# A decoder step's attention with its fills ordered by first use, and its softmax sums inverted inside it and loaded broadcast by the last projection

## What is computed

```
def one_block(args):
    q_i, cq_i, blk = args
    s = jnp.einsum('bqhd,bkhd->bhqk', q_i, k).astype(jnp.float32) * ATTN_SCALE
    s = s + cq_i[..., :, None] - ck[:, :, None, :]
    q_pos = blk * Q_BLOCK + jnp.arange(Q_BLOCK)
    mask = key_pos[None, :] <= q_pos[:, None]
    p = jax.nn.softmax(jnp.where(mask, s, -jnp.inf), axis=-1)
    return jnp.einsum('bhqk,bkhd->bqhd', p.astype(v.dtype), v)
...
yp = yp + (att * jax.nn.silu(g)) @ w_out1
```

## Time and profile before

| | us |
|---|---|
| median of 3 runs | 3041.19 (3039.72 to 3047.91) |
| profiled execution | 3042.56 |
| its span | 3040.8 |
| granted TensorE clock, mean | 0.967 of full |

### The profile page before, as it was taken

One profiled execution on the slowest core, in us unless ns is written; L12 is line 12 of the kernel. 1 busy time (PEld: TensorE's weight loads), 2 busy tenths in 40 slices (PEclk: granted clock), 3 DMA queues, 4 the chain that ended last, 5 costly groups with the idle time before them and its releaser, 6 DMA issues. The chain is left out here.

```text
span 3040.8 us, 46331 instructions
## 1 busy us (share of the span) xinstructions
PE 2789.8 (92%) x17133; PEld 2224.5 (73%) x17133; DVE 1592.0 (52%) x2154; ACT 1026.1 (34%) x1725; POOL 1377.5 (45%) x986
## 2 busy tenths in 40 slices
PE   3899999869989999999999739999999999998999
PEld 3899999757749989999899725555555555554887
DVE  4244333343545789865555465555645555453432
ACT  4333325312452222221122104454444455444100
POOL 0000000010003885469999836777776777776000
PEclk9999999979999999999999959999999999999999
DMA  4101111055635888788888767787897877874531
GB/s 122 44 28 47 46 35 37 14 182 173 183 119 170 293 288 276 252 276 272 268 261 275 220 152 221 207 242 217 218 252 205 240 211 221 238 212 140 168 119 63
DMA packets 327914, 547.68 MB, mean 180 GB/s; under 512 B 76093, under 2 KB 220129, under 8 KB 319212
## 3 DMA queue, kind: packets, MB, share of 16 engines
q1 hardware_dynamic: 246604, 454.31, 50.7%
q10 hardware_dynamic: 78080, 75.65, 7.6%
q0 software_dynamic: 3008, 14.81, 1.3%
HBM read 449.58 MB, written 95.12 MB: 179 GB/s over the span
## 5 line engine op out<-in xcount | busy, mean ns | idle before, releaser
L1174 POOL TENSOR_TENSOR p_kq<-p_kq 128x1024 f32<-128x1024 f32 x256 | 624.4, 2465 | 373.9 <-DMA p_kq<-in_cache_k_dram 373.5
L2037 POOL TENSOR_TENSOR at_acc<-at_acc,at_w 128x512 f32<-128x512 f32 (+3 forms) x576 | 645.2, 1120 | 229.5 <-ACT at_w L2165 165.7
L112 PE MATMUL p_pb<-p_w,x_xh 128*128 128x256 f32 x2048 | 593.0, 290 | 15.6 <-DVE p_w L1505 15.6
L2200 DVE TENSOR_REDUCE at_mx<-at_mx 128x1 f32<-128x512 f32 (+3 forms) x640 | 382.7, 608 | 427.2 <-PE at_mx L2072 311.9
L113 PE MATMUL p_pb<-p_w,x_xh 128*128 128x256 f32 x2048 | 580.3, 283 | 0.0
L114 PE MATMUL p_pb<-p_w,x_xl 128*128 128x256 f32 x2048 | 579.9, 283 | 0.0
L2165 ACT ACTIVATE at_w<-at_st,c_nckt 128x512 f32<-128x512 f32 (+3 forms) x640 | 389.6, 623 | 366.1 <-PE at_st L2098 193.2
L1607 DVE TENSOR_REDUCE p_sc<-p_kq 128x16 f32<-128x1024 f32 x256 | 310.0, 1216 | 201.6 <-POOL p_kq L1174 201.4
L112 PEld LDWEIGHTS p_pb<-p_w,x_xh 128*128 128x128 f32 x2048 | 391.2, 191 | 28.2 <-DVE p_w L1505 17.4
L113 PEld LDWEIGHTS p_pb<-p_w,x_xh 128*128 128x128 f32 x2048 | 392.9, 192 | 0.0
L114 PEld LDWEIGHTS p_pb<-p_w,x_xl 128*128 128x128 f32 x2048 | 392.1, 191 | 0.0
(11 more groups left out here) (296 smaller groups left out, 3802.9 us busy)
## 6 DMA issues: line engine op xcount, KB each, us to landing
p_kq<-in_cache_k_dram SPq DMA_DIRECT2D x256, 512.0 KB, 4.7
at_vp<-in_cache_v_dram SPq DMA_DIRECT2D x256, 512.0 KB, 5.2
o_mt<-mixed SPq DMA_DIRECT2D x32, 512.0 KB, 4.9
p_raw<-in_w_in_dram ACTq DMA_DIRECT2D x32, 512.0 KB, 5.8
at_q<-qh SPq DMA_DIRECT2D x32, 512.0 KB, 10.5
at_k<-kh SPq DMA_DIRECT2D x32, 512.0 KB, 8.2
l_raw<-in_w_in_dram SPq DMA_DIRECT2D x20, 512.0 KB
mixed<-l_w POOLq DMA_DIRECT2D x8, 1028.0 KB, 4.2
```

The source lines that it names most:

```text
L112: nc.tensor.matmul(out, lhs[0], rhs[0], start=(k == 0), stop=False)
L1174: nc.gpsimd.tensor_tensor(kq[:, slot[page]], kq[:, slot[page]], kq[:, slot[query]], ALU.mult).then_inc(kmul, 1)
L2037: nc.gpsimd.tensor_tensor(t[:, 512 - wd:512], t[:, 512 - wd:512], W[n % RW][:, 0:wd], ALU.add).then_inc(accd, 1)
L2200: nc.vector.reduce_max(mx[:, u % 2, j, seg:seg + 1], MX[r % 2][:, 0:wd], AX.X).then_inc(mread, 1)
```

## The change

In `attention`:

- The fills stand in the order of their first use, and each user waits for the one it needs. VectorE zeroes `KM` and `K2` of head 0 only, then rounds the mask; `KM` and `K2` of head 1 are zeroed behind the maxima of units 0 and 1. `Q2` is no longer zeroed: POOL fills its rows 64 to 127 with ones at once (they meet zeros in `KM` and `K2`). POOL begins with the mask. The rounding of the identity goes to ScalarE. The head mask's eight selections become entries `HM` of the list, one each six steps.
- The sums are inverted in place, in `lt`, by VectorE: new entries `OI`, eight per head, 64 columns each, one after each of the steps behind `LS`. SP stores them after that.

In `out1`: the table `ls`, `expand`, the reciprocals and `turn_out` are gone. Instead each tile's `load_mixed` also loads the inverted sums, each head's row broadcast over the 64 partitions of that head, in two transfers, and `divide` reads them from SBUF.

The diff, cut to its core:

```diff
+        for x in range(8):
+            side.setdefault(5 + 6 * x, []).append(("HM", x))
...
                             later.setdefault(n + 5, []).append(("LS", p[0] // NC))
+                            for x in range(DC):
+                                later.setdefault(n + 6 + x, []).append(("OI", x, p[0] // NC))
...
         sums(H - 1)
+        for x in range(DC):
+            seq.append(("OI", x, H - 1))
...
                 if x == 2 and h < 2:
-                    sp.wait_ge(padd, 3 * h + 2)
+                    sp.wait_ge(padd, 2 * h + 1)
...
             def store_sums(h):
-                sp.wait_ge(lsd, h + 1)
+                sp.wait_ge(linv, DC * (h + 1))
...
+            nc.gpsimd.memset(maskf[:], 0.0).then_inc(masked, 1)
...
+            nc.gpsimd.memset(Q2[0][HD:P].bitcast(F32), 1.0).then_inc(onesd, 1)
...
+            pool.wait_ge(padd, 2)
+            nc.gpsimd.memset(K2[0][HD:HR].bitcast(F32), 1.0).then_inc(made, 1)
...
+                elif w[0] == "HM":
+                    base, mult = ((0, 1), (HD - 1, -1))[w[1] // 4]
+                    hm = headmask[32 * (w[1] % 4):32 * (w[1] % 4) + 32, :]
+                    pool.wait_ge(hmd, w[1] + 1)
+                    pool.wait_ge(accd, added)
+                    nc.gpsimd.affine_select(out=hm, in_=hm, compare_op=ALU.is_ge, fill=0.0, base=base,
+                                            pattern=[[mult, z.D]], channel_multiplier=-mult * HD).then_inc(hmd, 1)
...
-            pe.wait_ge(made, 6)
-            pe.wait_ge(dvm, 2)
+            pe.wait_ge(dvm, 1)
+            pe.wait_ge(idm, 1)
...
+                            pe.wait_ge(made, (1, 6)[min(u // NC, 1)])
...
+            nc.scalar.activation(identr[:], C.ident[:], ACT.Copy).then_inc(idm, 1)
...
-            for s in range(2):
-                for t in (Q2, KM, K2):
-                    nc.vector.memset(t[s][HD:P].bitcast(F32), 0.0).then_inc(padd, 1)
-            dve.wait_ge(masked, 3)
+            nc.vector.memset(KM[0][HD:P].bitcast(F32), 0.0).then_inc(padd, 1)
+            nc.vector.memset(K2[0][HD:P].bitcast(F32), 0.0).then_inc(padd, 1)
+            dve.wait_ge(masked, 2)
             nc.vector.tensor_copy(maskr[:], maskf[:]).then_inc(dvm, 1)
-            nc.vector.tensor_copy(identr[:], C.ident[:]).then_inc(dvm, 1)
...
+                    if u < 2:
+                        nc.vector.memset((KM, K2)[u][1][HD:P].bitcast(F32), 0.0).then_inc(padd, 1)
...
+                elif w[0] == "OI":
+                    _, x, h = w
+                    cols = slice(512 // DC * x, 512 // DC * (x + 1))
+                    if x == 0:
+                        dve.wait_ge(lsd, h + 1)
+                    nc.vector.reciprocal(lt[:, cols], lt[:, cols]).then_inc(linv, 1)
...
+                for x in range(2):
+                    sp.dma_start(rb[x * z.HD:(x + 1) * z.HD, n % 3, :, 0:rows],
+                                 D.lsum[:, ds(col, rows)].rearrange("(k x) t -> x k t", x=2)[x].partition_broadcast(z.HD)).then_inc(r_in[n % 3], 16)
...
             def divide(n, rows):
-                dve.wait_ge(spread, n + 1)
+                dve.wait_ge(r_in[n % 3], 32 * (n // 3 + 1))
...
-            turn_out(*TILES[0])
             for n, rows, col in TILES:
-                if n + 1 < N:
-                    turn_out(*TILES[n + 1])
                 product(n, rows)
```

More of the change, by code:

```diff
@@ L1735, in width @@
         return 512 - P * max(0, kb - 4 * (u % NC))
+    DC = 8
     def first_odd(u):
@@ L1960, in _ @@
                     value_load(w[1])
-                elif w[0] in ("OF", "LS"):
-                    due.append([2, *w])
+                elif w[0] == "OF" or w[0] == "OI" and w[1] == DC - 1:
+                    due.append([2, w[0], w[-1]])
                 elif w[0] == "SD" and w[-1] < B - 1:
@@ L1995, in _ @@
         def _(pool):
-            for s in range(2):
[L1997 to L2000, removed]
+            nc.gpsimd.memset(maskf[:], 0.0).then_inc(masked, 1)
+            pool.wait_ge(masked, 1)
+            nc.gpsimd.affine_select(out=maskf[:], in_=maskf[:], compare_op=ALU.is_ge, fill=NEG, base=0,
+                                    pattern=[[-1, P]], channel_multiplier=1).then_inc(masked, 1)
@@ L2012, in _ @@
             nc.gpsimd.memset(onesh[:], 1.0).then_inc(made, 1)
-            pool.wait_ge(made, 6)
-            for base, mult, off in ((0, 1, 0), (HD - 1, -1, 0)):
-                for x in range(4):
-                    pool.wait_ge(masked, (3 if mult == 1 else 7) + x)
-                    hm = headmask[32 * x:32 * x + 32, :]
-                    nc.gpsimd.affine_select(out=hm, in_=hm, compare_op=ALU.is_ge, fill=0.0, base=base,
-                                            pattern=[[mult, z.D]], channel_multiplier=-mult * HD).then_inc(masked, 1)
@@ L2021, in _ @@
-            pool.wait_ge(masked, 11)
+            nc.gpsimd.memset(headmask[:], 1.0).then_inc(hmd, 1)
+            pool.wait_ge(made, 5)
+            pool.wait_ge(hmd, 1)
+            pool.wait_ge(padd, 4)
+            nc.gpsimd.memset(K2[1][HD:HR].bitcast(F32), 1.0).then_inc(made, 1)
+            pool.wait_ge(made, 6)
             added = 0
@@ L2356, in _ @@
         def _(dve):
-            def invert(n, rows, col):
-                nc.vector.reciprocal(rl[:, ds(col, rows)], ls[:, ds(col, rows)]).then_inc(recd, 1)
             def divide(n, rows):
-                dve.wait_ge(spread, n + 1)
+                dve.wait_ge(r_in[n % 3], 32 * (n // 3 + 1))
                 dve.wait_ge(m_in[n % 3], 16 * (n // 3 + 1))
@@ L2364, in divide @@
                     dve.wait_ge(m_lo, n - 1)
-                nc.vector.tensor_tensor(md[:, n % 2, :, 0:rows], mt[:, n % 3, :, 0:rows], rb[:, n % 2, :, 0:rows],
+                nc.vector.tensor_tensor(md[:, n % 2, :, 0:rows], mt[:, n % 3, :, 0:rows], rb[:, n % 3, :, 0:rows],
                                         ALU.mult).then_inc(divided, 1)
@@ L2402, in _ @@
         def _(pe):
-            def turn_out(n, rows, col):
-                pe.wait_ge(recd, n + 1)
-                if n >= 2:
-                    pe.wait_ge(divided, n - 1)
-                for k in range(z.KB):
-                    last = nc.tensor.matmul(rb[:, n % 2, k, 0:rows], expand[:, k * P:(k + 1) * P], rl[:, ds(col, rows)],
-                                            start=True, stop=True)
-                last.then_inc(spread, 1)
             def product(n, rows):
```

55 lines of the change are left out of this document (21 added, 34 removed).

## The result

| | us |
|---|---|
| after, median of 4 runs | 3091.82 (3089.14 to 3101.19) |
| before, beside it, median of 4 runs | 3044.13 (3039.72 to 3047.91) |
| ratio | 1.0165, 95% interval 1.0141 to 1.0189 |
| profiled execution of after | 3092.58, span 3090.9, mean granted clock 0.961 |

The change made the kernel 48 us slower. The forecast was 3025 us, the range 3000 to 3036, the chance of slower 0.09: it was wrong, and the time is outside the range.

What follows compares the result with a forecast made beforehand. TensorE was taken as the bound inside attention, DMA loads and fills at its entry, TensorE partly spreading sums in the last projection. -11.7 + 24.1 + 3.2 - 0.5 - 29.6 - 1.7 = -16.2 us gave 3025 us, range 3000 to 3036.

Steps and rivals of the forecast that it cites:

- The new loads move as much as that of `att`; they must fit in 11.1: Last projection, per tile: the added loads of sums were taken to fit in 11.1 us of DMA time beside 5.1 busy.
- -29.6 for the turns: Last projection: fifteen matmul steps spreading the inverted sums between products go, 14 x 1.98 + 1.88, saving 29.6 us.
- -1.7 for the dip: End of the last projection: without the narrow spreading for the sample rows, a low-clock stretch should not come, saving 1.7 us.
- -0.5 for the start: Start of the last projection: sums table, reciprocals and turning matmuls go, broadcast sums precede weights; -0.5 us, between -2 and +4.
- rival 3: Last projection: broadcast loads bind, 13.4 us of DMA per tile instead of 11.1, +32 on 14 tiles, 3057 us; chance 0.04.
- Entry: Entry of attention: TensorE starts after the third load instead of all fills, first scores 11.7 us earlier, bounds -8 to -12.
- Rival 4: Entry of attention: first three loads or the new fill come as late as before, up to 11.7 us given back; chance 0.07.
- Reciprocals in attention: Attention, behind each head's sums: waits for VectorE cost TensorE 1.0 us per even head, 2.3 per odd, +24.1 us in all.
- the replay of the ring: Attention: maxima matmuls wait on reduces through two buffers; stepping through them with reciprocals added gave 1.0 us per even head.
- Rival 1: Attention: VectorE, busy only 54%, hides the reciprocals; total gain then 40.3 us, 3001 us; chance 0.20.
- Rival 2: Attention: the two maxima buffers pass on nearly every reciprocal, 3.8 us per head, 56 instead of 24, 3057 us; chance 0.05.
- Last head: End of attention: the last eight reciprocals have no TensorE work covering them and delay the sums' store, +3.2 us.

Runs made afterwards that it cites:

- the run without broadcast loads: The change, but the last projection loads the inverted sums once and spreads them by TensorE as before; reciprocals stay in attention: 3060.04 us, ratio 1.0063.
- the run with the entry alone: Before plus only the change's fills, waits and head mask; no reciprocals in attention, last projection as before: 3033.37 us, ratio 0.9972.
- the run with distinct rows: The change, but the two loads per tile fetch rows of the attention output, each partition from its own address: 3029.25 us, ratio 0.9957.
- the spread run: The change with all 128 rows of sums stored and loaded, reciprocals three steps apart from 14 steps behind a head's end: 3006.70 us, ratio 0.9890.
- the replicas' run: The change, but attention stores all 128 partitions of inverted sums and the last projection loads each 32 partitions from 32 rows: 3029.42 us, ratio 0.9956.
- the run with both small repairs: The change with 512-column broadcast loads for four tiles and reciprocals three steps apart from 14 steps behind a head's end: 3014.34 us, ratio 0.9905.

## Why the prediction was wrong

**The step that failed** is the sentence "The new loads move as much as that of `att`; they must fit in 11.1", and the terms under it: -29.6 for the turns, -1.7 for the dip, -0.5 for the start. The turns did leave TensorE's work: with rows of their own for the loads the stage lost 31.1 us, with 2.8 more at its start. But I priced a load by its bytes, and by the DMA share of before, and these loads have another price: 1024 reads of 16 small places, some 14 ns each, 14 us per tile. That the price goes by reads, the runs show; whether the small place or the stride of zero makes it is not settled. In place of 10.9 us tiles came 13.1 to 15.6, in place of -31.8 came +29.4.

**The rival that came near** is the third. The earlier trace rows has a broadcast load of 512 KB at 8.3 us, and rival 3 took it as transfer time: 13.4 us per tile, at a chance of 0.04, "Against: other loads went with it". That the broadcast loads bind the stage came true; that 13.4 is near the measured 13.1 to 15.6 is luck. The row is a load of 4 KB read by 128 partitions, 128 reads, which at 14 ns are 1.8 us (an estimate from the price above). Its 8.3 us were mostly other loads, as the reading against it said: while it was under way, the DMA engines of before moved 3.0 MB, six times its size (window 627 to 635.4):

```profile
DMA packets 2563, 3.01 MB, mean 359 GB/s; under 512 B 137, under 2 KB 1923, under 8 KB 2563
```

The change makes 1024 reads of 512 bytes per tile. Counting reads instead of bytes would have made the two incomparable, and the bound open above. The rival's total of 3057 fell short by 35 us, about half of it because it had no price at the start of the stage: there the same reads stand ahead of the weights in one queue, and the first addition came 18.0 us later (2.8 with rows of their own), where my upper bound was +4.

**Entry.** Right: 11.1 of 11.7, released by the third load as the prediction says, and 10 us alone. The selections of the head mask and the moved fills were priced at zero; 1.4 us shows ahead of the first head's sums. Rival 4 did not come.

**Reciprocals in attention.** Size right (26.9 against 24.1), with 1.0 to 1.3 for even heads (1.0) and 2.3 to 2.6 for odd ones (2.3). For even heads the replay of the ring holds. For odd heads it was partly luck: the waits, forecast at 2.3 us, cost 1.7 where no dip of the clock came, and a dip, which the forecast did not have, made up the rest. Rival 1 (VectorE hides them) was wrong here and would have been right for heads 0 to 14 eleven steps later in the same list. Rival 2 (the ring passes on nearly all, 3.8 us per head) was wrong at 27 of 56 us. That the page "VectorE: DVE Perf Modes" of the Trainium skill, section on the TRN2 errata, would give 127 ns per reciprocal (an estimate from that page) is not borne out: the profile has 534.

**Last head**: +2.9 for +3.2. **Clock dip near the end**: I tied it to the narrow spreading of the sample rows. In the run without broadcast loads that spreading is there and the last two intervals are 12.98 and 10.88 us, without a dip; the run with the entry alone has it (14.58). So the reason was wrong, though in the run with distinct rows, without it, no dip came. The rule that the prediction cited from the Trainium skill, "TensorE: Matmul & The Clock Gate", Part 1 (sustained matmul activity releases the gate), was no danger here: product 0 began at the low clock with the turns ahead of it and without them, and its first ten matmuls took 4.4 us at the low level in both (in before and in the run with distinct rows).

## What to carry to other kernels

- Price a load by its reads and where they go, too, not by its bytes alone. Many partitions reading the same few hundred bytes of memory cost about 14 ns a read here, 512 bytes or 2 KB; fetch long runs, or store copies when an engine already holds them, and look for such a load in front of the weights in a queue.
- A busy share of 54% on an engine says nothing of eight instructions in a place. The same 64 us (120 reciprocals) cost 27 us right behind a head's end and next to nothing eleven steps later; before giving an operation up, move it along its list.
- The best here are the entry fills, copies in place of the broadcast and the reciprocals moved: 3005 to 3008 us, 1.1 to 1.2% under before, with the change's idea kept.

## What was not expected of the hardware

- The broadcast loads leave the DMA engines half idle (0.53 of a tile) while everything waits for them, so a low DMA share does not mean that transfers have room. The issue itself grows: 2.6 us in the median on SP's queue for one load, against 434 ns for that of `att` in before.
- 256 KB and 1 MB of the same rows land in 15.0 and 13.9 us; 32 bytes of offset between the readers bring 15.0 down to 8.0.
- The granted clock fell behind the pauses of all seven odd heads in after and of none in the spread run. But longer pauses don't decide it: behind head 1 of the replicas' run the same pauses as in after had no dip, while before has one behind head 7 and the run with both small repairs two, with pauses no longer than elsewhere. What decides it, these runs leave open.
- Open: where the reads queue up (in the memory, or on the way to it), and whether it takes the same place or the stride of zero, no run here shows: the only run with the same place and another stride also had its reads unaligned. That the price goes by reads does not depend on it.
